# A Strassen level on the input projection of heads 1 to 3 of a hybrid decode step

## What is computed

```python
xn = rmsnorm(x, norm_gain)
proj = jnp.einsum('btd,dp->btp', xn, w_in)
gb, gc, hc, zc, q, k, v, o, zm, ig, fg = jnp.split(proj, np.cumsum(PROJ_SPLITS)[:-1].tolist(), axis=-1)
yc, conv_new = short_conv(gc * hc, conv_buf, conv_w)
y_conv = gb * yc * jax.nn.silu(zc)
qh, kh, vh = heads(q), heads(k) * (HEAD_DIM ** -0.5), heads(v)
h, state = mlstm_seq(qh, kh, vh, igh, lfh, state)      # chunks of 128 tokens
h = h * lax.rsqrt(jnp.mean(h * h, axis=-1, keepdims=True) + EPS)
y_m = (h * mh_norm_gain * jax.nn.sigmoid(o)) * jax.nn.silu(zm)
out = jnp.einsum('btw,wd->btd', jnp.concatenate([y_conv, y_m], axis=-1), w_out)
return rmsnorm(x + out, final_norm_gain)               # and the new states
```

## Time and profile before

| | us |
|---|---|
| median of three runs | 1104.28 (1104.0 to 1104.38) |
| span of the profiled execution | 1100.9 |
| TensorE busy | 1061.1 (96%) |
| VectorE busy | 540.9 (49%) |
| ScalarE busy | 340.7 (31%) |
| GpSimd busy | 257.9 (23%) |

### The profile page before, as it was taken

How to read it: one execution, slowest core, us unless ns; L and a number is a source line. 1 busy time by engine, 2 the same in 40 slices (tenths; PEclk the granted TensorE clock), 3 DMA queues, 4 the chain that set the end, 5 groups by cost and what they waited for, 6 DMA issues and landing times. The chain is left out here.

```text
span 1100.9 us, 17978 instructions
## 1 busy us (share of the span) xinstructions
PE 1061.1 (96%) x7180; PEld 602.0 (55%) x7180; DVE 540.9 (49%) x1008; ACT 340.7 (31%) x672; POOL 257.9 (23%) x333
## 2 busy tenths in 40 slices
PE   3999999999999999999999999999999999999995
PEld 3655546565666555656665556566655555444442
DVE  5786664556553434575534345655332323434333
ACT  6636434243402232434022324340213131111111
POOL 5012313021211323212113232121111121542422
PEclk9999999999999999999999999999999999999998
DMA  9484532033200322342003224310212062365651
GB/s 243 135 182 78 132 86 49 24 107 101 89 22 17 96 63 77 93 110 89 21 17 96 64 77 120 102 32 22 93 43 86 25 220 91 108 223 205 233 201 77
DMA packets 124184, 108.74 MB, mean 99 GB/s; under 512 B 42384, under 2 KB 109092, under 8 KB 124100
## 3 DMA queue, kind: packets, MB, share of 16 engines
q1 hardware_dynamic: 88192, 68.83, 22.0%
q0 software_dynamic: 7600, 25.03, 6.2%
q10 hardware_dynamic: 28308, 13.73, 4.8%
HBM read 65.43 MB, written 33.41 MB: 90 GB/s over the span
## 5 line engine op out<-in xcount | busy, mean ns | idle before, releaser
L800 PE MATMUL bank<-xTh,Wh 128*128 128x512 f16 (+2 forms) x1304 | 421.2, 342 | 5.7 <-DVE Wl L163 5.7
L801 PE MATMUL bank<-xTl,Wh 128*128 128x512 f16 (+2 forms) x1304 | 423.9, 342 | 0.0
L802 PE MATMUL bank<-xTh,Wl 128*128 128x512 f16 (+2 forms) x1304 | 423.6, 342 | 0.0
L802 PEld LDWEIGHTS bank<-xTh,Wl 128*128 128x128 f16 x1304 | 129.2, 99 | 120.3 <-issue 0.7
L800 PEld LDWEIGHTS bank<-xTh,Wh 128*128 128x128 f16 x1304 | 129.2, 99 | 113.4 <-DVE Wl L163 6.0
L801 PEld LDWEIGHTS bank<-xTl,Wh 128*128 128x128 f16 x1304 | 129.3, 99 | 108.8 <-issue 2.4
L809 PE MATMUL bank<-Wh,xTh 128*128 128x128 f16 x544 | 92.8, 219 | 0.6 <-DVE ysum L163 0.6
L811 PE MATMUL bank<-Wh,xTl 128*128 128x128 f16 x544 | 92.8, 219 | 0.0
L810 PE MATMUL bank<-Wl,xTh 128*128 128x128 f16 x544 | 92.8, 219 | 0.0
L163 ACT ACTIVATE tz<-bank 128x512 f32<-128x512 f32 x32 | 19.1, 598 | 148.4 <-PE bank L802 147.7
L672 POOL TENSOR_TENSOR ysumst<-ysum,ysumst 128x1024 f16<-128x1024 f32 x16 | 34.1, 2130 | 105.5 <-ACT ysumst L163 105.5
(11 more groups left out here) (336 smaller groups left out, 1520.5 us busy)
## 6 DMA issues: line engine op xcount, KB each, us to landing
wst<-in_w_in ACTq DMA_DIRECT2D x23, 512.0 KB, 3.9
xs<-in_x_prompt SPq DMA_DIRECT2D x22, 512.0 KB, 4.3
y_ops<-ysumst POOLq DMA_DIRECT2D x16, 512.0 KB, 3.2
w_ops<-xs SPq DMA_DIRECT2D x16, 448.0 KB, 4.5
wst<-in_w_in SPq DMA_DIRECT2D x13, 512.0 KB, 5.5
out<-xs POOLq DMA_DIRECT2D x11, 512.0 KB, 2.9
Wh<-y_ops SPq DMA_DIRECT2D x12, 448.0 KB, 3.6
Wl<-y_ops SPq DMA_DIRECT2D x12, 448.0 KB, 4.4
```

What stands on the lines that cost most here:

```text
L800: mm(out, wh[:, k, :], xh, start=(k == 0), stop=False)
L801: mm(out, wh[:, k, :], xl, start=False, stop=False)
L802: last = mm(out, wl[:, k, :], xh, start=False, stop=(k == KT - 1))
```

## The change

The four pairs (K, Q), (GC, HC), (GB, ZC) and (O, ZM) of heads 1 to 3 are each taken as one 2 x 2 product: the two tiles by the two halves of the model dimension on the weights' side, the two halves of the model dimension by the two halves (256 tokens) of a block on the tokens' side. Strassen's scheme in Winograd's form takes seven products of quarters in place of eight, each twelve matmuls of 256 columns. V stays as it was, in quarters. Head 0 is not changed in its products.

- TensorE: `pair` runs M1, M5, M6, M2, M7, M3, M4 into three banks, XB, QB and YB (banks 0, 2, 1). M6 adds onto a copy of XB in YB, M7 onto a sum in QB, M4 onto YB after it has been read. The mixed tokens use the same weight operands: the first tile of a pair as before, the second (`mixed_second`) with 36 matmuls in place of 24.
- Tokens: in head 0 `store_tokens` writes the plain quarters to `x_ops` in DRAM, and sixteen units of `token_sums` (GpSimd, five operations each) with a high and a low part make four sums. From head 1 on `load_operands` brings a block's eight operands (4 MB, two alternating places) into `xTh` and `xTl`, whose old contents are no longer needed.
- Weights: GpSimd multiplies the tiles with the norm's factors (`gain_raw`, nine a head; VectorE does seven of head 1's) and forms four sums a pair in place (`weight_sums`). Seventeen splits a head (`split_high`, `split_low`) give the operands. Splits 0 to 10 stand in the last block of the head before, 11 to 16 in the head's first block.
- ScalarE and VectorE: `seed` and `fifth` (ScalarE) copy XB to YB and QB to SBUF, `seed` (VectorE) writes the sum into QB, `second_of_second` reads YB. Evacuations are of half tiles (256 columns).
- The slabs' operations are cut into a plain part and a sums part, and GpSimd's sums are made in place.
- The output weights' operands lie elsewhere in SBUF and are loaded accordingly.

More of the change, by code:

```diff
@@ L128, in t1, with s_t0, s_t1 @@
     return ordinal(t1_uses, T1_PRO, g, b, name, first)
+T0_HEAD = T0_PRO + sum(len(t0_uses(b, True)) for b in range(NB))
+T1_HEAD = T1_PRO + sum(len(t1_uses(b, b < NB - 1)) for b in range(NB))
+T1_STREAM = ["args", "kv", "score", "num", "oz", "hT", ("state", 0), ("state", 1), ("state", 2)]
+def s_t0(n, name):
+    return T0_HEAD + 2 * (n - NB) + (name == "kT")
+def s_t1(g, name):
+    return T1_HEAD + (g - 1) * len(T1_STREAM) + T1_STREAM.index(name)
 def tok0(b):
@@ new lines, in stream_chunk @@
+            def stream_chunk(g, b, c):
+                n = nth(g, b)
+                out = N[c // 2][:, (c % 2) * DV1:(c % 2 + 1) * DV1]
+                if c == 0:
+                    pe.wait_ge(s_free, n * 3 + 1)
+                    pe.wait_ge(q_scaled, n + 1)
+                    pe.wait_ge(q_free, q_uses(g, b, 1))
+                    if b == 0:
+                        pe.wait_ge(cn_meta, g + 1)
+                        pe.wait_ge(ma_free, g)
+                else:
+                    pe.wait_ge(a_free if c % 2 else s_free, n * 3 + 2 + (c - 1) // 2)
+                if c == 2 and b == 0:
+                    pe.wait_ge(mb_free, g)
+                mm(out, dp[:, c * P:(c + 1) * P], v1[:, c, :], start=True, stop=False)
+                last = mm(out, eh[:, c * P:(c + 1) * P], cn[:, :], start=False, stop=True)
+                if c == CH - 1:
+                    last.then_inc(n_full, 1)
+                kv, full, free = ((S, s_full, s_free), (A, a_full, a_free))[1 - c % 2]
+                pe.wait_ge(free, n * 3 + 1 + c // 2)
+                mm(kv[:, 0:DV1], kw[:, c * P:(c + 1) * P], v1[:, c, :], start=True, stop=True).then_inc(full, 1)
@@ new lines, in mixed_second @@
+            def mixed_second(out, p):
+                for k in range(KT):
+                    if k < KT // 2:
+                        parts = [[w[:, PAIRS[p][0], k, :] for w in W], [w[:, k, :] for w in T14[p]]]
+                    else:
+                        parts = [[w[:, k - KT // 2, :] for w in B22[p]]]
+                    xh, xl = xTh[:, k, 0:MIX], xTl[:, k, 0:MIX]
+                    for i, (wh, wl) in enumerate(parts):
+                        mm(out, wh, xh, start=(k == 0 and i == 0), stop=False)
+                        mm(out, wh, xl, start=False, stop=False)
+                        last = mm(out, wl, xh, start=False, stop=(k == KT - 1))
+                return last
@@ new lines, in head_squares, with exps @@
+            def head_squares(n, chunks_):
+                act.wait_ge(rec_ready, n + 1)
+                for c in chunks_:
+                    last = fn(junk2[:, 0:P], N[c // 2][:, (c % 2) * DV1:(c % 2) * DV1 + P], ACT.Square,
+                              scale=rec[:, c:c + 1], accum_out=hss[:, c:c + 1])
+                    if c < CH - 1:
+                        did(last)
+                    else:
+                        mark(last.then_inc(h_sq, 1), h_sq, n + 1)
+            def exps(n, out, src, kind, done, value):
+                for c in range(CH):
+                    cc = slice(c * P, (c + 1) * P)
+                    last = fn(out[:, cc], src[:, cc], ACT.Exp, bias=sel[:, c, kind:kind + 1])
+                    if c < CH - 1:
+                        did(last)
+                mark(last.then_inc(done, 1), done, value)
@@ new lines, in first_half, with second_half, stream_block @@
+            def first_half(t):
+                return t[:, 0:HALF]
+            def second_half(t):
+                return t[:, HALF:BT]
+            def stream_block(g, b):
+                n, B = nth(g, b), blk(g, b)
+                m = [pair_no(g, b, p) for p in range(4)]
+                prep = g + 1 if b == NB - 1 and g < H - 1 else None
+                late = g if b == 0 else None
+                slab = SLAB_FIRST[g, b] if (g, b) in SLAB_FIRST else None
+                if b == NB - 1 and g < H - 1:
@@ new lines, in head_norms @@
+            def head_norms(n):
+                dve.wait_ge(n_full, n + 1)
+                for i in range(2):
+                    nv = N[i][:, 0:2 * DV1].rearrange("p (c v) -> p c v", c=2)
+                    did(copy(den[:, 2 * i:2 * i + 2], nv[:, :, P]))
+                did(stt(den[:, :], den[:, :], -1.0, den[:, :], ALU.mult, ALU.max))
+                did(tt(den[:, :], den[:, :], sel[:, :, 0], ALU.max))
+                mark(reciprocal(rec[:, :], den[:, :]).then_inc(rec_ready, 1), rec_ready, n + 1)
```

1166 lines of the change are left out of this document (944 added, 222 removed).

## The result

The changed kernel takes 1255.23 us (median of four runs, 1252.78 to 1256.06) where the kernel before takes 1104.14 (1102.99 to 1104.38): 1.136 times as long, interval 1.1344 to 1.1377. The prediction had the sign; its 1136 us and its upper bound of 1170 were far too low. The profiled execution took 1256.06 us with a span of 1254.3.

The account below looks back on a forecast made before the run. TensorE, busy for 96% of the span, was taken to bound the kernel. In us: 1104.3 - 57 (columns) + 5 (mixed tokens) + 55 (waits) + 13 (slabs) + 8 (head 0) + 8 (clock) = 1136, range 1065 to 1170.

Parts of the forecast that it names:

- columns saved: Twelve blocks of heads 1 to 3: seven products for eight save 4.8 us a block, 57 us (47 to 62).
- mixed tokens: Heads 1 to 3: the second tile of each pair takes 36 matmuls where it took 24, adding 5 us.
- hand-offs: Between the three banks of each pair: hidden under a product's 1.31 us, so put at nothing.
- walked waits and slabs, heads 1 to 3: TensorE waiting behind GpSimd's chains in first and last blocks, 55 us, and in slab blocks, 13 us.
- head 0: Token sums on GpSimd and token stores on SP's queue in head 0: 8 us, bounds 0 and 18.
- clock: Granted clock falling to 0.50 after five of ten waits over 4 us: some 8 us (0 to 25).
- The rival of failing hand-offs: All 144 bank hand-offs 0.4 us over their cover: 58 us more, 1170 to 1195 us; chance 0.06.
- M5 of pair 1: First block of a head: 4.2 us wait, as ScalarE's copy of V stands behind a split.
- Mixed pair 3: First block of a head: 5.4 us wait ahead of pair 3, whose sums wait for the mixed tokens' mean.
- M6 of pair 2: Last block of heads 1 and 2: 7 us wait, as ScalarE's seed stands behind a split.
- Two engines on one memory: VectorE's splits beside GpSimd's work take turns: 12 us more at full turns, an upper bound left out of the sum.
- The faster rival: GpSimd's chains fit in first and last blocks: 1052 to 1101 us; below 52 us of waits the change wins; chance 0.30.

Follow-up runs that it names:

- e3: The changed kernel with the slab loads ahead of the block's operand loads on SP's queue; 1235.31 us.
- e1: The changed kernel with head 0's token sums on GpSimd formed on a small part of their columns; 1230.57 us.
- e5: The changed kernel with SP's token stores behind the transpositions and the first block's operand loads ahead of head 1's weights; 1247.02 us.
- e7: The changed kernel with GpSimd doing the powers first in blocks 1 and 2 of head 0 and token sums in the gaps; 1246.54 us.
- e9: The changed kernel with slab loads first, SP's, the splits' and GpSimd's orders changed, and token sums, weight sums and GpSimd's factors shortened; 1145.93 us.
- e13: The changed kernel with short sums and factors, and two-input GpSimd work of about the left-out length behind each; 1238.6 us.
- e17: The changed kernel with short sums and factors, and GpSimd memsets of about the left-out length behind each; 1229.32 us.
- e14: The changed kernel with short sums and factors, and GpSimd memsets of about the left-out length ahead of each; 1263.57 us.
- e12: The kernel before with nine GpSimd subtractions of 512 columns that nothing waits for in the last block of heads 0 to 2; 1126.25 us.
- e15: The kernel before with twelve GpSimd memsets that nothing waits for in the last block of heads 0 to 2; 1103.98 us.

## Why the prediction was wrong

By its own terms, in us; measured idle time is length less TensorE's busy time in the stretches above.

| term | predicted | measured |
|---|---|---|
| columns saved | -57 | 5.1 and 4.8 a clean block: as predicted |
| mixed tokens | +5 | not seen apart |
| hand-offs | 0 | 0 |
| walked waits and slabs, heads 1 to 3 | 55 + 13 | 40 + 41 + 12 = 93 |
| head 0 | 8 | 55 (idle 65.2, before 9.8) |
| clock | 8 | 49 (50.8 less 1.7) |

These give 145 of the 153 us between the spans; the time ahead of head 0's first V product adds 1, and some 7 stay unassigned. Of the 119 us that the prediction was too low, head 0 is 47, the clock 41, the walk with the slabs 25.

- **The products and their hand-offs: right.** Starts 0.109 apart, blocks of 48.1 and 46.7 us without waits. The rival of failing hand-offs is out (the argument against it counted seven blocks with splits or slabs; there are nine); TensorE's time was there to be had, and was.
- **The walk: right in its places, somewhat small.** M5 of pair 1: 4.2 predicted, 4.7, 5.2 and 5.2 measured. Mixed pair 3: 5.4, and three times 6.3. M6 of pair 2: 7, and 5.4. Pair 1 of the last block: 1, and 2.5. From the last block into the next: 5, and 2.1 + 4.3. Added up, 63 for 55. The slabs missed the most, 26 for 13: the operand loads were put at nothing, since they "have a whole block", which looked at the loads themselves and not at what SP's queue holds behind them (e3: 20 us of the total).
- **Head 0: the step that failed by the mechanism.** I wrote "0 (TensorE's next need comes after) and 18; I take 8, near GpSimd's still fitting into its block". It was costed by whether GpSimd's work fits, though I had just argued for the heads that order counts and not fit. Each token operand is a chain over GpSimd, ScalarE and VectorE, and VectorE stands in order too. The wait at 180.48, on VectorE and then TensorE:

```profile
165.18 2.16 DVE L203 TENSOR_TENSOR fgain<-wst,fgain 128x1024 f16<-128x1024 f32 x1 [6.32 <-ACT fgain L203]
...
171.84 3.21 DVE L203 TENSOR_TENSOR_SCAN u<-gatebuf,mst,auxbuf 4x512 f32<-4x512 f32 x1
...
180.07 0.35 DVE L203 SCALAR_TENSOR_TENSOR cn<-cn,sel,bank 128x129 f32<-128x129 f32 x1
```

```profile
180.48 0.80 PE L1154 MATMUL bank<-v,dp 128*128 128x129 f32 x2 [14.94 <-DVE cn L203]
```

  VectorE waits 6.3 us for a token unit's high part, the state's scan stands behind it and takes 3.2 us beside GpSimd where it took 1.27 in the kernel before, and TensorE's state step comes 14.9 us late. e1, e5 and e7 make head 0 some 26, 4 and 7 us shorter. In e9, without the sums' length, its four blocks still take 76.8, 68.6, 62.7 and 81.6 us (76.8, 62.2, 57.2 and 52.9 in the kernel before), and the 12.4 us behind the store out of a single buffer stand in the last: a cost of its own.
- **The clock: the term that was mis-sized, 8 for 49, beyond its bound of 25.** I let only half of the waits over 4 us drop it, at 1.7 us each. In the trace shorter ones drop it too (head 1's wait of 1.8 us at 441.66 is followed by 3.4 us at half pace), and behind a long one the half pace lasted 2.7 to 5.9 us, 1.3 to 2.9 lost. Head 0's waits, which the sum hardly had, brought 13 us of it.
- **Two engines on one memory: left out of the sum, with a bound of 12.** e13 against e17 says 9, and in e14, where the reading is gone, it gave nothing back. In the kernel before, where nothing else is late, it is 22 (e12 against e15).
- **The faster rival** rested on GpSimd's 37 us of free time in each block. It has free time still (37% busy) and is what ends the chains. Its turning point, 52 us of waits, was passed nearly three times over (151 us more idle time).

What stays open: the 43 us of e9 above before lie nearly all in head 0, which is idle for 25 us more than before and loses 10 more to the clock; some 5 are head 1's work ahead of the mark. In heads 1 to 3 what the products save and what waits and clock take about cancel. How much of head 0 the splits, the stores and the order would each give back no run tells.

## What to carry to other kernels

An engine with free time isn't a free engine: work put into an in-order queue costs by what stands behind it and by who waits for that, on every block that it passes, also those that gain nothing from the change, as head 0 here. Fewer multiplications pay where the operands can be prepared without anyone waiting for them; here a block saved 5 us, and heads 1 and 2 lost 57 and 55 to waits and the clock (40.2 + 17.1 in head 1). Where TensorE is the bound, count the clock behind a wait with it: here 49 us came on top of 151 of waits. And when waits are filled to keep the clock up, the filling has to end before the wait does.

## What the chip showed that I had not expected

- GpSimd's work slows VectorE's state scan, which has 4 partitions and two inputs, as it does wide work. The groups of the kernel before, of after, and of e1, where only the token sums are short (busy, mean ns):

```profile
L163 DVE TENSOR_TENSOR_SCAN u<-restart,mst,arow 4x512 f32<-4x512 f32 x4 | 5.1, 1272 | 0.1
```

```profile
L203 DVE TENSOR_TENSOR_SCAN u<-gatebuf,mst,auxbuf 4x512 f32<-4x512 f32 x4 | 7.6, 1894 | 0.1
```

```profile
L203 DVE TENSOR_TENSOR_SCAN u<-gatebuf,mst,auxbuf 4x512 f32<-4x512 f32 x4 | 5.1, 1272 | 0.1
```

- A memset of 1024 16-bit columns on GpSimd beside VectorE costs nothing that can be measured (12.22 us of them a block, +1.5 in all), while subtractions of about the same length cost 22 us more.
- Where 3.5 MB stood ahead of them on the queue, the slabs' loads of 256 KB landed 10.2 us after their issue (median of 16), for 4.6 in the kernel before.
